# A hybrid encoder step on one core: order of work around the convolution and in the prologue

## The reference

```python
def rms_norm(x, g):
    y = x * lax.rsqrt(jnp.mean(x * x, axis=-1, keepdims=True) + EPS)
    return y * g

# layer 0: h = rms_norm(x, g) @ w_in (1024 x 3088), attention and GLA, out projection, MLP
# layer 1:
def conv_module(xn, buf, w1, b1, w_dw, b_dw, ln_g, ln_b, w2, b2):
    u = xn @ w1 + b1                                    # 1024 -> 2048
    u = u[..., :D_MODEL] * jax.nn.sigmoid(u[..., D_MODEL:])
    full = jnp.concatenate([buf.astype(u.dtype), u], axis=1)
    y = depthwise_conv(full, w_dw) + b_dw               # causal, 31 taps for each channel
    y = jax.nn.silu(layer_norm(y, ln_g, ln_b))
    return y @ w2 + b2, full[:, -(CONV_W - 1):]         # also the last 30 rows
```

## Time and profile before

| | before |
|---|---|
| median of 3 runs | 1392.53 us (1390.88 to 1393.76) |
| the profiled execution | 1393.9 us, its span 1392.2 us |
| TensorE matmul busy | 1356.1 us, 97% of the span |
| VectorE busy | 722.3 us, 52% |
| ScalarE busy | 468.2 us, 34% |
| GpSimd busy | 81.6 us, 6% |
| chain that ended last | TensorE 88%, VectorE 6%, ScalarE 4% |
| mean granted TensorE clock | 0.996 |

### The profile page before, as it was taken

How to read it: one execution, slowest core, us unless ns; L and a number is a source line. 1 busy time by engine, 2 the same in 40 slices (tenths; PEclk the granted TensorE clock), 3 DMA queues, 4 the chain that set the end, 5 groups by cost and what they waited for, 6 DMA issues and landing times.

```text
span 1392.2 us, 26754 instructions
## 1 busy us (share of the span) xinstructions
PE 1356.1 (97%) x11210; PEld 1283.0 (92%) x11210; DVE 722.3 (52%) x1034; ACT 468.2 (34%) x743; POOL 81.6 (6%) x116
## 2 busy tenths in 40 slices
PE   6999999999999999999999999988999999999998
PEld 5999788779999999999998988867999999999998
DVE  6684568675544334334335789976544333334322
ACT  4221555534333123123123433236343213213121
POOL 5100100001100000000011000001100000000000
PEclk9999999999999999999999999999999999999999
DMA  5422410222222322222220222201222322222221
GB/s 170 156 73 87 148 32 1 82 83 92 86 89 78 99 75 91 91 91 91 91 90 32 80 80 71 80 17 61 91 74 79 97 84 91 91 91 91 91 77 49
DMA packets 105554, 115.61 MB, mean 83 GB/s; under 512 B 3725, under 2 KB 102648, under 8 KB 105209
## 3 DMA queue, kind: packets, MB, share of 16 engines
q1 hardware_dynamic: 102585, 101.46, 22.9%
q0 software_dynamic: 2816, 12.84, 2.9%
q10 hardware_dynamic: 64, 0.02, 0.0%
HBM read 104.61 MB, written 7.21 MB: 80 GB/s over the span
## 4 chain that ended last, share of the span: by engine, by line
PE 88%; DVE 6%; ACT 4%; issue 1%; DMA 1%; POOL 0%; SPq 0%; ACTq 0%; DVEq 0%; POOLq 0%
PE ps L978 70%; PE ps L1348 4%; PE ps L1111 4%; DVE rstd L1544 2%; PE ps L1128 1%; PE ps L1222 1%; PE ps L959 1%; PE ps L1161 1%; PE ps L1145 1%; PE ps L1001 1%; ACT w_h L578 1%; PE ps L963 1%; DVE w_l L1452 1%; PE ps L1358 1%; ACT xn L898 1%
## 5 line engine op out<-in xcount | busy, mean ns | idle before, releaser
L578 ACT ACTIVATE w_h<-w_raw 128x2048 fp32r<-128x2048 f32 x92 | 175.3, 1906 | 274.0 <-PE ps L978 270.6
L1452 DVE TENSOR_TENSOR w_l<-w_raw,w_h 128x2048 fp32r<-128x2048 f32 x92 | 211.7, 2302 | 106.4 <-ACT w_h L578 106.4
L978 PE MATMUL ps<-x_h,w_h 128*128 128x272 f32 x1216 | 256.5, 292 | 7.7 <-DVE resid L1790 3.4
L978 PE MATMUL ps<-x_h,w_l 128*128 128x272 f32 x1216 | 253.2, 290 | 0.0
L978 PE MATMUL ps<-x_l,w_h 128*128 128x272 f32 x1216 | 252.7, 290 | 0.0
L978 PE MATMUL ps<-xf_h,w_h 128*128 128x272 f32 x1024 | 212.2, 288 | 0.0
L978 PE MATMUL ps<-xf_h,w_l 128*128 128x272 f32 x1024 | 212.2, 289 | 0.0
L978 PE MATMUL ps<-xf_l,w_h 128*128 128x272 f32 x1024 | 211.3, 288 | 0.0
L978 PEld LDWEIGHTS ps<-x_h,w_h 128*128 128x128 f32 x1216 | 193.1, 190 | 13.5 <-issue 6.3
L978 PEld LDWEIGHTS ps<-x_l,w_h 128*128 128x128 f32 x1216 | 193.0, 190 | 0.0
L978 PEld LDWEIGHTS ps<-x_h,w_l 128*128 128x128 f32 x1216 | 191.6, 190 | 0.0
(11 more groups left out here) (259 smaller groups left out, 1636.9 us busy)
## 6 DMA issues: line engine op xcount, KB each, us to landing
w_raw<-in_w_ffn_up SPq DMA_DIRECT2D x32, 1024.0 KB, 5.4
w_raw<-in_w_ffn_down SPq DMA_DIRECT2D x32, 1024.0 KB, 5.1
w_raw<-in_w_in_ab SPq DMA_DIRECT2D x12, 1024.0 KB, 5.3
w_raw<-in_c_w_pw SPq DMA_DIRECT2D x12, 1024.0 KB, 5.7
w_raw<-in_w_out_ab SPq DMA_DIRECT2D x4, 1024.0 KB, 5.3
glu_swap<-glu POOLq DMA_DIRECT2D x16, 151.5 KB, 2.7
resid_scratch<-resid POOLq DMA_DIRECT2D x1, 2176.0 KB, 7.6
resid<-resid_scratch POOLq DMA_DIRECT2D x1, 2176.0 KB, 8.9
```

The source lines that it names most:

```text
L578: act.activation(w_h[s][:], w_raw[:, s], ACT.Copy).then_inc(w_hi, 1)
L978: ins = pe.matmul(ps[:, 2 * m + t, 0:HALF], a[s][:, k, w], b[:, k, t * HALF:(t + 1) * HALF], start=(k == 0 and q == 0), stop=(k == KT - 1 ...
L1452: dve.tensor_tensor(w_l[s][:], w_raw[:, s], w_h[s][:].bitcast(F32), ALU.subtract).then_inc(w_lo, 1)
```

## The change

It does six things.

1. **Prologue, order.** VectorE copies all eight residual tiles first, then splits weight 0, then makes the eight `x_l`. ScalarE rounds weight 0 after tile 1, not after tile 3. Unit 0 runs through `together` (both output tiles for each k), and the mean square stands ahead of its last k. The parameters are transposed on TensorE behind unit 0 and copied out on VectorE behind unit 0's read-out; `wlr_h` and `wlr_l` are made later still. ScalarE loads the table of the root ahead of the root.
2. **Prologue, filling matmuls.** 16 `keep_clock` matmuls as soon as `ones` is set, then 14, 6, 2, 2 between the transposes of k = 0.
3. **First unit of U_PW1** runs through `together` too.
4. **Last channel tile.** `glu_conv` is cut in three, and the glu of tile 7 is made ahead of the sum of tile 6. Tile 7 has 8 pairs of taps on TensorE (128 matmuls) and 15 taps on VectorE. The means of tiles 0 to 2 stand ahead of the taps of tile 7, the other five behind.
5. **Edge rows.** They are transposed behind the variance (a wait for `cv_std`), into PSUM banks 4 to 7, and copied by VectorE behind the first read-out of U_PW2; the two stores wait for that on GpSimd's queue, ahead of its sums of squares. The waits of ScalarE and VectorE for the stores move to the start of the last MLP. The filling matmuls there go from 30 to 12.
6. **Second weight of U_PW2.** ScalarE rounds it right behind the last sigmoid, and VectorE splits it inside the loop over j, at j = 3.

```diff
 def tile0(u):
-    return 8 + 2 * u + (2 if u >= U_PW2 else 0)
+    return 8 + 2 * u
+    def tap_pairs(m):
+        return [(t, t + PAIRS) for t in range(PAIRS)] + ([LAST_PAIR] if isinstance(m, int) and m == KT - 1 else [])
@@ gpsimd
-        pool.wait_ge(slot_free[0], tile0(U_PW2) // 2)
-        pool.wait_ge(slot_free[1], tile0(U_PW2) // 2)
+        pool.wait_ge(edges_out, 2)
@@ scalar
-            if k == 3:
+            if k == 1:
                 split_hi(0, 0, 0)
             square(0, k, k % 2, slot_free[k % 2], k // 2 + 1)
-        act.wait_ge(vec_ready, 1)
-        act.activation(wlr_h[:, :, 0:RANK], wlr[:], ACT.Copy).then_inc(wlr_hi, 1)
+        act.activation(no_use[:], eps[:], ACT.Sqrt)
...
+            if u == 0:
+                act.wait_ge(vec_ready, 1)
+                act.activation(wlr_h[:, :, 0:RANK], wlr[:], ACT.Copy).then_inc(wlr_hi, 1)
...
-        act.wait_ge(gemm_done, tile0(U_PW2) - 1)
-        act.activation(ccn[:, 0, :], flat(0)[0:PAD, :], ACT.Copy).then_inc(slot_free[0], 1)
-        act.wait_ge(gemm_done, tile0(U_PW2))
-        act.activation(ccn[:, 1, :], flat(1)[0:PAD, :], ACT.Copy).then_inc(slot_free[1], 1)
+        split_hi(U_PW2, 0, 1)
         act.activation(no_use[:], eps[:], ACT.Sqrt)
@@ tensor
+        pe.wait_ge(ones_ready, 1)
+        keep_clock(16, 6)
...
                 if k == 0:
+                    keep_clock((0, 14, 6, 2, 2)[c], 6)
                     pe.wait_ge(x_landed[c], 16)
...
-        x_ready = lambda k: pe.wait_ge(xl_ready, X_MIX0 + k + 1)
-        unit(0, 0, 0, x_h, x_l, x_ready, mean_square)
+        def x_ready(k):
+            if k == KT - 1:
+                norm(0)
+            pe.wait_ge(xl_ready, X_MIX0 + k + 1)
+        together(0, 0, x_h, x_l, x_ready)
+        parameters()
...
-        gated(0, 0)
+        together(U_PW1, 0, x_h, x_l, lambda k: pe.wait_ge(xl_ready, X_MIX1 + k + 1))
         gated(0, 1)
...
         add_taps(KT // 2 - 1, 0)
-        for n in range(2):
-            pe.wait_ge(slot_free[n], tile0(U_PW2) // 2 - 1)
-        for n in range(2):
-            at = SEQ if n == 0 else SEQ + PAD + DEC
-            for k in range(KT):
-                ins = pe.transpose(flat(n)[0:PAD, k * P:(k + 1) * P], glu[:, k, at:at + PAD], ident[:])
-            ins.then_inc(gemm_done, 1)
         pe.wait_ge(slot_free[0], tile0(U_PW2) // 2)
-        for k in range(KT - 2):
+        for k in range(3):
             add_mean(k)
         add_taps(KT // 2 - 1, 1)
-        add_mean(KT - 2)
+        for k in range(3, KT):
+            add_mean(k)
         pe.wait_ge(slot_free[1], tile0(U_PW2) // 2)
-        add_mean(KT - 1)
...
-        keep_clock(30, 2)
+        pe.wait_ge(cv_std, 2)
+        for n in range(2):
+            at = SEQ if n == 0 else SEQ + PAD + DEC
+            for k in range(KT):
+                ins = pe.transpose(flat(2 + n)[0:PAD, k * P:(k + 1) * P], glu[:, k, at:at + PAD], ident[:])
+            ins.then_inc(edges_T, 1)
+        keep_clock(12, 2)
@@ vector
-        for k in range(KT + 1):
-            if k < KT:
-                dve.wait_ge(gemm_done, k + 1)
-                dve.tensor_copy(resid[:, k, :], flat(k % 2)[:, 0:TOK]).then_inc(slot_free[k % 2], 1)
-            if k == 5:
-                split_lo(0, 0, 0)
-            if k:
-                dve.wait_ge(slot_free[(k - 1) % 2], (k + 1) // 2)
-                lo_gain(k - 1, X_MIX0, x_l, x_h, V_MIX)
+        for k in range(KT):
+            dve.wait_ge(gemm_done, k + 1)
+            dve.tensor_copy(resid[:, k, :], flat(k % 2)[:, 0:TOK]).then_inc(slot_free[k % 2], 1)
+        split_lo(0, 0, 0)
+        for k in range(KT):
+            dve.wait_ge(slot_free[k % 2], k // 2 + 1)
+            lo_gain(k, X_MIX0, x_l, x_h, V_MIX)
...
-        glu_conv(KT // 2 - 1, 0)
-        glu_conv(KT // 2 - 1, 1)
+        gated_frames(KT // 2 - 1, 0)
+        conv_taps(KT // 2 - 1, 0)
+        gated_frames(KT // 2 - 1, 1)
+        conv_sum(KT // 2 - 1, 0)
+        conv_taps(KT // 2 - 1, 1)
+        conv_sum(KT // 2 - 1, 1)
...
                 cv_scaled(j + 2)
-        dve.wait_ge(stored, 16 * 8)
-        phase(U_PW2, 4, add_resid(U_PW2, V_B2, X_FFN1, V_FFN + 8))
+            if j == 3:
+                split_lo(U_PW2, 0, 1)
+        def edges():
+            for n in range(2):
+                dve.wait_ge(edges_T, n + 1)
+                dve.tensor_copy(ccn[n], flat(2 + n)[0:PAD, :]).then_inc(edges_out, 1)
+        phase(U_PW2, 4, add_resid(U_PW2, V_B2, X_FFN1, V_FFN + 8), ahead=edges)
```

More of the change, by code:

```diff
@@ L578, in split_hi, with phase @@
             act.activation(w_h[s][:], w_raw[:, s], ACT.Copy).then_inc(w_hi, 1)
-        def phase(u0, units, evacuate, first=None):
-            if first:
+        def phase(u0, units, evacuate, first=None, ahead=False):
+            if first or ahead:
                 for s in range(2):
-                    split_hi(u0, 0, s + 1)
-                    if s == 0:
+                    if s or not ahead:
+                        split_hi(u0, 0, s + 1)
+                    if first and s == 0:
                         first()
                     evacuate(0, s)
-            with act.Fori(1 if first else 0, units // 2) as i:
+            with act.Fori(1 if first or ahead else 0, units // 2) as i:
                 for s in range(2):
@@ L901, in _ @@
             act.activation(x_h[:, k, cv_span(c)], xn[:, j % 3, cv_span(c)], ACT.Copy).then_inc(cv_hi, 1)
-        act.wait_ge(stored, 16 * 8)
-        phase(U_PW2, 4, squares_of(3, U_PW2, V_FFN + 8))
+        phase(U_PW2, 4, squares_of(3, U_PW2, V_FFN + 8), ahead=True)
         def y_out(u):
@@ L927, in _, with keep_clock @@
     def _(pe):
+        def keep_clock(n, bank):
+            any_bits = ones[:].bitcast(mybir.dt.bfloat16)
+            for _ in range(n):
+                pe.matmul(ps[:, bank, 0:2 * P], any_bits[:, 0:P], any_bits, start=True, stop=True)
+        pe.wait_ge(ones_ready, 1)
+        keep_clock(16, 6)
         pe.wait_ge(gains_landed, 32)
@@ L1326, in gated @@
                 pe.wait_ge(slot_free[m], i * 2 + tile0(U_PW1 + d) // 2)
-                first = isinstance(i, int) and i + d + m == 0
-                tile(s, m, x_h, x_l, (lambda k: pe.wait_ge(xl_ready, X_MIX1 + k + 1)) if first else None)
+                tile(s, m, x_h, x_l)
         def add_taps(i, d):
@@ L1335, in add_taps @@
             pe.wait_ge(swapped[s], (i + d // 2) * 32 + 32)
+            pairs = tap_pairs(m)
             pe.wait_ge(conv_ready, m + 1)
             x = glu[:, m, :]
-            for t in range(PAIRS):
+            for pair in pairs:
                 for c in range(2):
@@ L1348, in add_taps @@
                             ins = pe.matmul(sum_ps(r, CH)[to, c, :], diag[rows, s, tap, :], src,
-                                            start=(t == 0), stop=(t == PAIRS - 1))
+                                            start=(pair is pairs[0]), stop=(pair is pairs[-1]))
             ins.then_inc(taps_done, 1)
@@ L1452, in split_lo, with phase @@
             dve.tensor_tensor(w_l[s][:], w_raw[:, s], w_h[s][:].bitcast(F32), ALU.subtract).then_inc(w_lo, 1)
-        def phase(u0, units, evacuate, first=None):
-            if first:
+        def phase(u0, units, evacuate, first=None, ahead=None):
+            if first or ahead:
                 for s in range(2):
-                    split_lo(u0, 0, s + 1)
-                    if s == 0:
+                    if s or not ahead:
+                        split_lo(u0, 0, s + 1)
+                    if first and s == 0:
                         first()
                     evacuate(0, s)
-            with dve.Fori(1 if first else 0, units // 2) as i:
+                    if ahead and s == 0:
+                        ahead()
+            with dve.Fori(1 if first or ahead else 0, units // 2) as i:
                 for s in range(2):
```

128 lines of the change are left out of this document (72 added, 56 removed).

## The result

| | before | changed |
|---|---|---|
| median | 1393.05 us (1390.88 to 1393.76, 4 runs) | 1379.75 us (1379.25 to 1382.43, 4 runs) |
| ratio to before, 95% interval | | 0.9914 (0.9901 to 0.9927) |
| the profiled execution | 1393.9 us, span 1392.2 | 1382.43 us, span 1380.7 (the longest of its four) |
| TensorE matmul busy | 1356.1 us, 97% | 1353.3 us, 98% |
| chain that ended last | TensorE 88%, VectorE 6%, ScalarE 4% | TensorE 91%, VectorE 4%, ScalarE 3% |

What follows compares the result with a forecast made beforehand. The prediction took TensorE, 88% of the chain of waits, as the bound. Its terms, -0.6 - 2.0 - 6.8 - 2.3 = -11.7, taken from 1392.5, gave 1380.8 us, range 1378 to 1386.

Steps and rivals of the forecast that it cites:

- the upper bound: Whole kernel: the slow end of the terms, +2.8 - 2.0 - 6.2 - 0.8 = -6.2, giving 1386.3 us.
- Prologue: Start to unit 1: faster transposes and copies first, unit 1 at 40.75 against 41.29; -0.6 us (-1.8 to +2.8).
- All that follows hangs on unit 1, so the shift passes through: End of the prologue: the shift in unit 1's start, taken as -0.6 us, carries on to all later work.
- rival "slower": Units 0 and 1: matmuls stay at 0.222, losing 5.7 and 9.0 us; 1395.5 us, chance 0.02.
- First rival: Prologue: transposes stay at the slow rate despite fillers, so the prologue costs 2.8; 1384.2 us, chance 0.25.
- First unit of U_PW1: At U_PW1: the second unit starts at 768.9 on the sigmoid instead of 770.9; -2.0 us (-3.4 to 0).
- Last channel tile: Last channel tile: earlier glu, means filling TensorE's wait, edge transposes off the path; -6.8 us (-7.1 to -6.2).
- the tight one: Last channel tile: the swap, landing at 908.0 against means until 908.1; 0.9 later would cost 0.6 us.
- U_PW2: At U_PW2: stall of 2.0 at j = 6, but earlier second unit and no 0.50 behind it; -2.3 us (-2.3 to -0.8).
- The rival that the stall itself brings the 0.50: U_PW2 loop: slow clock after j = 3's stop, 1.5 us plus 1 catching up; about 1383, chance 0.10 shared with a late swap.
- Late parts: The three terms behind the prologue, at U_PW1, the last channel tile and U_PW2: -2.0, -6.8 and -2.3 us.

Runs made afterwards that it cites:

- again: The changed kernel run and profiled a second time with no edit; 1380.46 us, ratio 0.9908.
- old_prologue: The changed kernel with the prologue of before, everything from the first unit of U_PW1 on as changed; 1380.26 us, ratio 0.9904.
- the fillers at 140: Changed kernel plus early sigmoid table, U_PW2 split ahead of its loop, more prologue fillers, fillers between k's turned rows and before gate means, `lr_ready` wait moved; 1375.90 us.
- no_fillers: The changed kernel without the 16 + 24 filling matmuls in front of and among the first transposes; 1383.77 us, ratio 0.9933.
- first_pw1_as_before: The changed kernel with only the first unit of U_PW1 put back: m = 0 waiting for each x_l, then m = 1; 1382.82 us, ratio 0.9922.

## Why the prediction was right, and where it was not

**The result.** 1379.75 lies in the range, 1.05 below the forecast. The likeliest case came, and no rival came at its price. The sum was right partly by luck, because errors cancel: the prologue gave nothing, and stretches that the change doesn't touch were shorter. Three slips in the working decide nothing: 40.75 and 39.6 against 41.29 are -0.5 and -1.7, not -0.6 and -1.8; the upper bound takes -2.0 for U_PW1 where its own worst case was 0, so it should have been 1388.3; and 256 columns against 272 at 0.128 give 0.12 for a filler, not 0.11 (twelve took 1.47).

**Prologue (forecast -0.6, measured 0).** Almost each event came where the text put it: the last copy 17.74 (17.5), five transposes 0.81 (0.8), unit 0 at 21.86 (21.6), the mean at 35.09 (34.6), unit 1 at 41.25 (40.75). In the seven profiles with this prologue unit 1 starts between 39.06 and 41.25. In three of them the chain comes from the transfer of x and VectorE's first copy starts at 9.7 to 9.9; in the other four, `again` among them, it comes from the transfer of the gains through the fillers of k = 0, and the first copy starts at 10.9 to 11.3. So fillers that ran late cost up to 1.6, where I had given them nothing, and under 1 if late. The average start is 40.3, 1.0 ahead of the one profile of before, and still nothing is left of it at 153, where the seven average 153.4, against 153.18 before and 153.61 in `old_prologue`. The step that failed is "All that follows hangs on unit 1, so the shift passes through". The forecast let TensorE stand for 2 us ahead of unit 1 behind narrow transposes and didn't ask for its clock. Unit 1 then starts at the 0.50 level and takes 13.71 and 13.62 where it took 12.26, and 14.8 to 15.0 in three others of the seven profiles. This is the rival "slower" at a sixth of its price: I had given unit 1's slow matmuls all or nothing. The second half of the failure lies further on. The stretches from unit 1 to 153 come to 111.9 before and to 112.8 to 113.5 in twelve of the thirteen later profiles, whatever the prologue; only the fillers at 140 break this, with 111.05. A profile that is slow for longer in unit 1 (60.0 to 60.1 to the q/k mean, four of them) has no slow stretch at 144 to 150 and needs 52.8 to 53.0 next; the three that are not slow in unit 1 (57.4) need 55.8 to 56.1. So in these profiles time won in unit 1 is given back there. Why before, with one profile, has 1.2 less than `old_prologue` in this stretch (113.3), with the same order of work, is open.

**First rival.** The transposes came at the fast rate. By the Trainium skill (TensorE: Matmul & The Clock Gate, "What's actually happening") the slow level is the default and activity releases it. The trace agrees that something must release it: without the fillers 37 transposes ran at 1.28 for five, with them at 0.81. But transposes alone did not release it, in 9.8 us of them without a stop.

**First unit of U_PW1 (-2.0, measured -1.6; undone, +1.6 to +1.7).** The mechanism is as told: the second unit starts 13.73 behind the first x_l, 13.6 forecast, behind a table load. The step is right, a little over-sized.

**Last channel tile (-6.8, measured -7.08).** The glu ends 0.6 ahead of tile 6's taps; the second swap, issued at 904.17, lands at 906.7 by the 2.5 that the view of this tile shows, just ahead of the third mean's end at 907.10. It was the tight one, as told, and held nothing. Taps 7.93 (8.0). The runs split the 7.1: 5.1 hang on the order of glu and sum, 1.4 on the sixteenth tap; some 0.5 is left for the rest, the edge transposes among it, which weren't tried alone. Parts that are undone one at a time need not add up, so this split is an estimate.

**U_PW2 (-2.3, measured -2.74 and -2.37).** The stall at j = 6 came with its size (ScalarE waits 1.84, TensorE 1.91; 2.0 forecast), the second unit starts 29.66 behind the variance (29.75), and behind its stop of 0.59 the clock is at its full level. The rival that the stall itself brings the 0.50 came in part: the level is there at 940 to 942 in the first profile and not in `again`, whose matmuls behind the same stop of 1.91 go at 0.125 each. Of the ten profiles with this stall seven show it and three don't, and the second unit starts 29.66 to 29.70 behind the variance in all ten. So it cost nothing where the rival gave 1.5 and 1: TensorE made it up before j = 15.

**The rest.** Late parts forecast -11.1; the profile shows -11.4 and some -0.5 in the last MLP, for which no term stood. The stretch to the norm of U_PW1 is 1.2 and 2.7 shorter, though nothing in it was changed. The chain of waits has one row that tells how: the same 2976 matmuls before,

```profile
365.34 372.84 PE ps L978 x2976
```

in the changed kernel,

```profile
366.54 372.01 PE ps L977 x2976
```

and in its second profile,

```profile
365.68 370.35 PE ps L977 x2976
```

All twelve profiled executions of the study and the one ahead of it show 372.0 or 370.4, and nothing between; before, with one profile, shows 372.8. So up to 1.7 us of any comparison of two profiles is this, and it can be part of what the medians have beyond the forecast. What sets the level is open. Slow stretches come elsewhere too: `old_prologue`, at 372.0, has 594.17 from the turned rows to the norm of U_PW1, 1.2 more than the changed kernel at the same pace, with a mean clock of 0.96 from 280 to 320 where the changed kernel has 1.00.

## What to carry to other kernels

On a kernel that TensorE bounds, take the order of two short groups on another engine as seriously as a large block: moving one glu ahead of one sum gave 5 of 13 us, since it took away a stop and the slow matmuls behind it. Price a stop of TensorE like these (1.9 to 4.9 us) twice, as the stop and as the slow matmuls that may follow (behind the stop of 1.91 they came in seven profiles of ten), and follow a saving ahead of such a place down the trace until another slow stretch has had its chance to take it back. Where effects are smaller than the spread between executions, cut the chain of waits at instructions that all versions share and compare the stretches.

## What the hardware showed that I had not expected

- The granted clock is recorded as 1.00 in the first 20 us, while the transposes of `no_fillers` run at 1.28 for five and the same ones at 0.81 behind fillers. In `no_fillers` it is still 1.00 from 24 to 28, where unit 0 runs at 0.226 a matmul; in the changed kernel it reads 0.50 for that rate at 22 to 24. Early in an execution the duration of a known matmul tells the rate, the record doesn't.
- Much of the spread of before goes with TensorE's mean clock: of the 11 executions beside `again`, the two at 0.997 and 0.998 have spans of 1389.1 and 1389.5, the two at 0.993 and 0.994 have 1393.8 and 1393.7. It is no general rule: the six of `no_fillers`, all at 0.996, lie between 1379.6 and 1383.3, and in `first_pw1_as_before` the lowest clock, 0.993, has the shortest span.
- The slow stretches of TensorE trade with each other: slow for longer at 41 to 46, none at 144 to 150, and the other way round, with a sum that moves by 0.7 only in the twelve profiles named above. The one of before lies 0.9 below them. What ties the two stretches together isn't shown.
- At a granted clock of 1.00 the long row of matmuls has two paces, 370.4 and 372.0 for 2976, in executions of one and the same code.
- An x_l beside GpSimd's sums takes 1.87 and a sum 1.66, against 0.78 and 1.36 apart. By the Trainium skill (SBUF — State Buffer, "SBUF: two separate sides") the one blocks the other for a whole instruction. The pace of a pair, 1.79, is shorter than 0.71 and 1.36 one behind the other, so the trace agrees with turns that overlap a little. Which part of an instruction overlaps it doesn't show, and a recorded duration may hold time on either side of the turn.
